# Three of the eight key/value units of the memory move: one into the differential attention's sub-layer norm, two round the query norm

## What is computed

```python
h = rmsnorm(x, g_mix_pre); proj = h @ w_in              # q, k, v, u
da = diff_attention(q, k, v, lam)                       # 4 heads, 2 blocks of 128 queries
da = rmsnorm(da, g_subln) * (1.0 - lam_init)            # the sub-layer norm, per head
mix = jnp.concatenate([da, po], axis=-1) @ w_out        # po: the pooled half, made earlier
x = x + rmsnorm(mix, g_mix_post)
hq = rmsnorm(x, g_x_pre)                                # the query norm
xq = (hq @ w_xq).reshape(b, s, X_HEADS, X_HEAD_DIM)
kv = (mem_n @ w_xkv).reshape(b, MEM_LEN, 2, X_HEADS, X_HEAD_DIM)   # depends on mem alone
sc = einsum(xq, kv[:, :, 0]); xo = einsum(softmax(sc), kv[:, :, 1])
```

## Time and profile before

| | before |
|---|---|
| median of 3 runs | 1147.33 us |
| the profiled execution, its own time | 1145.42 us |
| its span in the trace | 1143.6 us |
| PE busy | 1104.4 us (97%) |
| DVE busy | 628.3 us (55%) |
| ACT busy | 499.0 us (44%) |
| POOL busy | 33.2 us (3%) |
| mean granted TensorE clock | 0.994 of full speed |
| kv0 starts / first xq unit starts | 71.99 / 167.39 us from the span's start |

### The profile page before, as it was taken

The page is one execution under the profiler, slowest core; times in us unless marked ns, Lnnn a source line. Parts: engine busy times, 40 slices in busy tenths (PEclk is TensorE's granted clock), DMA queues, the critical chain, the costliest instruction groups (busy, mean ns, idle before and its releaser), DMA issues.

```text
span 1143.6 us, 18870 instructions
## 1 busy us (share of the span) xinstructions
PE 1104.4 (97%) x7892; PEld 1018.2 (89%) x7892; DVE 628.3 (55%) x831; ACT 499.0 (44%) x627; POOL 33.2 (3%) x47
## 2 busy tenths in 40 slices
PE   6999989999999999999999999999999999999997
PEld 6999779789999879988779999888999979999986
DVE  5765555364545445676565545446467565545542
ACT  5645455364444335554354444335532145444431
POOL 0100110000000001000010000000000010000000
PEclk9999989999999999999999999999999999999999
DMA  8833325334545546432135454554543233454530
GB/s 316 319 121 132 133 107 184 111 134 180 196 171 202 202 148 242 148 113 109 38 111 221 151 216 152 217 187 158 194 143 111 75 146 148 152 217 154 215 111 37
DMA packets 26718, 183.58 MB, mean 161 GB/s; under 512 B 3008, under 2 KB 3152, under 8 KB 5408
## 3 DMA queue, kind: packets, MB, share of 16 engines
q1 hardware_dynamic: 24912, 175.47, 42.4%
q0 software_dynamic: 1744, 7.20, 1.8%
HBM read 181.61 MB, written 1.05 MB: 160 GB/s over the span
## 4 chain that ended last, share of the span: by engine, by line
PE 92%; DVE 3%; ACT 2%; POOL 1%; issue 1%; DMA 1%; POOLq 0%; SPq 0%; DVEq 0%
PE G L1458 21%; PE G L1460 20%; PE G L1459 20%; PE D L1458 6%; PE D L1459 6%; PE D L1460 6%; PE D L1969 3%; PE D L1531 1%; POOL s_rstd L340 1%; PE D L1828 1%; PE D L1856 1%; ACT s_y L423 1%; DMA s_cst<-in_consts 1%; PE T L1841 1%; DVE s_xTl L841 0%
## 5 line engine op out<-in xcount | busy, mean ns | idle before, releaser
L812 DVE TENSOR_TENSOR s_wlo<-s_raw,s_whi 128x2048 fp32r<-128x2048 f32 (+1 forms) x165 | 371.8, 2276 | 179.5 <-ACT s_whi L412 179.5
L1458 PE MATMUL G<-s_xTh,s_whi 128*128 128x256 f32 x1448 | 408.7, 282 | 3.6 <-DVE s_xTl L841 3.6
L412 ACT ACTIVATE s_whi<-s_raw 128x2048 fp32r<-128x2048 f32 (+1 forms) x165 | 313.5, 1909 | 213.3 <-PE G L1460 108.0
L1460 PE MATMUL G<-s_xTh,s_wlo 128*128 128x256 f32 x1448 | 406.6, 281 | 0.0
L1459 PE MATMUL G<-s_xTl,s_whi 128*128 128x256 f32 x1448 | 405.9, 280 | 0.0
L1458 PEld LDWEIGHTS G<-s_xTh,s_whi 128*128 128x128 f32 x1448 | 272.0, 188 | 5.4 <-issue 5.2
L1459 PEld LDWEIGHTS G<-s_xTl,s_whi 128*128 128x128 f32 x1448 | 271.9, 188 | 1.0 <-issue 0.9
L1460 PEld LDWEIGHTS G<-s_xTh,s_wlo 128*128 128x128 f32 x1448 | 271.9, 188 | 0.1
L930 DVE TENSOR_TENSOR s_hb<-G,s_sg 128x512 f32<-128x512 f32 x33 | 22.8, 692 | 181.7 <-PE G L1460 145.3
L1458 PE MATMUL D<-s_whi,s_hTh 128*128 128x512 f32 x264 | 104.5, 396 | 0.0
L1459 PE MATMUL D<-s_wlo,s_hTh 128*128 128x512 f32 x264 | 104.1, 395 | 0.0
(11 more groups left out here) (309 smaller groups left out, 1134.2 us busy)
## 6 DMA issues: line engine op xcount, KB each, us to landing
s_raw<-in_stream SPq DMA_DIRECT2D x165, 1024.0 KB, 5.0
s_gb<-in_rows POOLq DMA_DIRECT2D x4, 512.0 KB, 4.1
s_xn<-in_x SPq DMA_DIRECT2D x2, 512.0 KB, 4.0
s_y<-in_mem POOLq DMA_DIRECT2D x1, 1024.0 KB, 11.5
s_w<-in_cmpw POOLq DMA_DIRECT2D x1, 1024.0 KB, 7.3
out<-s_y SPq DMA_DIRECT2D x4, 256.0 KB, 2.0
s_poolm<-in_poolm POOLq DMA_DIRECT2D x1, 768.0 KB, 15.1
s_retd<-in_retm POOLq DMA_DIRECT2D x1, 768.0 KB, 5.2
```

The source lines that it names most:

```text
L412: nc.scalar.activation(whi[:, u % RING, 0:n], raw[:, u % RING, 0:n], ACT.Copy)\
L812: nc.vector.tensor_tensor(wlo[:, u % RING, 0:n], raw[:, u % RING, 0:n], whi[:, u % RING, 0:n], ALU.subtract).then_inc(lo_ready, 1)
L1458: nc.tensor.matmul(out_, sh, mh, start=start, stop=False)
L1460: return nc.tensor.matmul(out_, sl, mh, start=False, stop=stop)
```

## The change

The units of the stream are reordered: kv0 to kv4, out0, out1, kv5, out2, out3, kv6, kv7, then xq as before. `sum_at` maps the four out units to their new places, `LATE_UNIT` the three late kv units.

- PE works through the attention in pairs of steps: four kv units (kv1 to kv4) instead of seven between eight steps, then out0 after the last transposes.
- kv5 runs between out1 and `head_transposes`, into bank T0. kv6 runs after out3 into D0, kv7 after the transposes of the query norm into D1. ACT copies each out in `late_kv_evac`, with a semaphore of its own, `kv_late`, that the first `x_scores` waits for.
- The query norm's transposes use D2, D3, T0, T1, and the two `keep_clock` matmuls ahead of them are gone.
- ACT and DVE do their steps in pairs too, with one split per pair, and the other splits are put at the places where the units now go.

```diff
-PHASES = [("in", 8), ("kv", 8), ("out", 4), ("xq", 4), ...
+PHASES = [("in", 8), ("kv", 5), ("out", 2), ("kv5", 1), ("out2", 2), ("kv6", 2), ("xq", 4), ...
...
 # ACT
-            for s in range(8):
-                if s < 7:
-                    kv_evac(s + 1)
-                act.wait_ge(sem("da_tr"), s + 1)
...
-                if s < 6:
-                    exps(s + 2)
-                if s < 7:
-                    split(kv0 + 1 + s + RING)
+            for h in range(4):
+                kv_evac(h + 1)
+                for s in (2 * h, 2 * h + 1):
+                    act.wait_ge(sem("da_tr"), s + 1)
...
+                if h < 3:
+                    exps(2 * h + 2)
+                    exps(2 * h + 3)
+                split(kv0 + 1 + h + RING)
 
             act.wait_ge(sem("da_nat"), 8)
...
-            split(BASE["out"] + RING)
+            split(sum_at("out", 0) + RING)
+            split(sum_at("out", 1) + RING)
+            late_kv_evac(5)
             for hp in range(2):
                 act.wait_ge(sem("da_T"), hp + 1)
...
-            split(BASE["out"] + 1 + RING)
+            split(LATE_UNIT[5] + RING)
             post_squares(0, "out", 2)
-            norm(2, BASE["out"] + 3, range(1, 4))
+            norm_squares(2, xn, lambda c: chunk(y, c), 1, range(1, 4))
+            split(sum_at("out", 2) + RING)
+            late_kv_evac(6)
+            norm_hi(2, xTh)
+            split(sum_at("out", 3) + RING)
+            split(LATE_UNIT[6] + RING)
+            late_kv_evac(7)
+            split(LATE_UNIT[7] + RING)
 # DVE
-            for s in range(8):
-                if s >= 1:
-                    da_copy(s - 1)
-                if s < 6:
-                    maxes(s + 2)
-                if s < 6:
-                    split(kv0 + 1 + s + RING)
-                    probs(s + 2)
+            for h in range(4):
+                if h >= 1:
+                    da_copy(2 * h - 2)
+                    da_copy(2 * h - 1)
+                if h < 3:
+                    maxes(2 * h + 2)
+                    maxes(2 * h + 3)
+                    probs(2 * h + 2)
+                    probs(2 * h + 3)
+                split(kv0 + 1 + h + RING)
+            da_copy(6)
             da_copy(7)
...
-            norm_rest(2, BASE["out"] + 3)
+            norm_mean(2, "x1", 1)
+            norm_diag("x1", 1)
+            split(sum_at("out", 2) + RING)
+            norm_lo(2, xTh, xTl)
+            split(sum_at("out", 3) + RING)
+            split(LATE_UNIT[6] + RING)
+            split(LATE_UNIT[7] + RING)
 # PE
+            def late_kv(j):
+                wait_unit(LATE_UNIT[j])
+                rows(LATE_UNIT[j], memTh, memTl, o=late_kv_bank(j)).then_inc(unit_done, 1)
...
-                if 2 <= n <= 4:
+                if 3 <= n <= 4:
                     keep_clock(o[3], 2)
...
-            for s in range(8):
-                if s < 7:
-                    unit(kv0 + s + 1, columns if s < 3 else rows, memTh, memTl)
-                else:
-                    pe.wait_ge(sem("da_max"), 8)
-                    sum_unit("out", 0, late=True)
-                if s >= 1:
-                    da_out(s - 1)
-                da_transposes(s)
-                if s < 6:
-                    da_scores(s + 2)
+            for h in range(4):
+                unit(kv0 + h + 1, columns if h < 3 else rows, memTh, memTl)
+                if h >= 1:
+                    da_out(2 * h - 2)
+                    da_out(2 * h - 1)
+                if h < 3:
+                    da_scores(2 * h + 2)
+                    da_scores(2 * h + 3)
+                da_transposes(2 * h)
+                da_transposes(2 * h + 1)
+            pe.wait_ge(sem("da_max"), 8)
+            sum_unit("out", 0, late=True)
+            da_out(6)
             da_out(7)
...
             sum_unit("out", 1)
+            pe.wait_ge(sem("da_nat"), 7)
+            late_kv(5)
             head_transposes(lambda t, h: un[:, t, P * h:P * h + P], (sem("da_normed"), 1), sem("da_T"), 2)
             for j in range(2):
                 pe.wait_ge(sem("da_lo"), j + 1)
                 sum_unit("out", 2 + j)
+            late_kv(6)
             norm_transposes(2)
+            late_kv(7)
...
                 if h == 0:
                     pe.wait_ge(sem("xT_ready"), 24)
+                    pe.wait_ge(sem("kv_late"), 3)
```

More of the change, by code:

```diff
@@ L49 @@
 GU, DN = 2 * (FF // 256), FF // 256
-PHASES = [("in", 8), ("kv", 8), ("out", 4), ("xq", 4), ("xo", 4), ("gu0", GU), ("dn0", DN),
+PHASES = [("in", 8), ("kv", 5), ("out", 2), ("kv5", 1), ("out2", 2), ("kv6", 2), ("xq", 4), ("xo", 4), ("gu0", GU), ("dn0", DN),
           ("ev", 14), ("eo", 4), ("gu1", GU), ("dn1", DN), ("od", 16), ("oo", 4),
@@ L65, with sum_at @@
 PAIRS = {"out": (2, 3, 0, 1), "xo": (0, 1, 2, 3), "eo": (2, 3, 0, 1), "oo": (0, 1, 2, 3)}
-N_OF = dict(PHASES)
+N_OF = dict(PHASES, out=4)
+LATE_UNIT = {5: BASE["kv5"], 6: BASE["kv6"], 7: BASE["kv6"] + 1}
+def sum_at(ph, j):
+    return BASE["out2"] + j - 2 if ph == "out" and j >= 2 else BASE[ph] + j
+LATE_KV = ("kv5", "out2", "kv6")
 POW_N = {"subln": 8, "gn": 8, "hg0": 8, "hg1": 8}
@@ L104, in bank_reads @@
     for name, count in PHASES:
-        if not name.startswith("gu") and name not in SUMS:
+        if not name.startswith("gu") and name not in SUMS and name not in LATE_KV:
             for j in range(min(max(u - at, 0), count)):
@@ L557, in kv_evac, with late_kv_evac @@
                     evac(kv0 + j, vx[:, :, 256 * (j - 4):256 * (j - 3)])
+            def late_kv_evac(j):
+                act.wait_ge(unit_done, LATE_UNIT[j] + 1)
+                nc.scalar.activation(vx[:, :, 256 * (j - 4):256 * (j - 3)], halves(late_kv_bank(j)[:]), ACT.Copy)\
+                    .then_inc(sem("kv_late"), 1)
             kv_evac(0)
@@ L562, in _ @@
             exps(1)
-            for s in range(8):
-                if s < 7:
-                    kv_evac(s + 1)
-                act.wait_ge(sem("da_tr"), s + 1)
[L567 to L571, removed]
-                if s < 6:
-                    exps(s + 2)
-                if s < 7:
-                    split(kv0 + 1 + s + RING)
+            for h in range(4):
+                kv_evac(h + 1)
+                for s in (2 * h, 2 * h + 1):
+                    act.wait_ge(sem("da_tr"), s + 1)
+                    if s >= 2:
+                        act.wait_ge(sem("da_out"), s - 1)
+                    n = P * (s % 2 + 1)
+                    nc.scalar.activation(aT[:, s % 2, 0:n], TB[s % 2][:, 0:n], ACT.Copy).then_inc(sem("aT"), 1)
+                if h < 3:
+                    exps(2 * h + 2)
+                    exps(2 * h + 3)
+                split(kv0 + 1 + h + RING)
             act.wait_ge(sem("da_nat"), 8)
@@ L1085, in _ @@
             mean_square("subln", ss[:, 32:40], P)
-            split(BASE["out"] - 1 + RING)
+            split(sum_at("out", 0) + RING)
             dve.wait_ge(rstd_ready, pow_at("subln") + 1)
@@ L1493, in gates, with rows @@
                 return ins
-            def rows(u, act_h, act_l, ready=None):
+            def rows(u, act_h, act_l, ready=None, o=None):
                 hi = whi[:, u % RING, 0:UNIT].rearrange("p (k n) -> p k n", k=KT)
@@ L1503, in rows @@
                         c = slice(P * t, P * t + P)
-                        ins = passes(G[bank(u)][:, 256 * t:256 * t + 256], (act_h[:, kt, c], act_l[:, kt, c]),
+                        ins = passes((G[bank(u)] if o is None else o)[:, 256 * t:256 * t + 256], (act_h[:, kt, c], act_l[:, kt, c]),
                                      (hi[:, kt, :], lo[:, kt, :]), kt == 0, kt == KT - 1)
@@ L1539, in sum_unit @@
                 act_l = xTl if act_l is None else act_l
-                u, last = BASE[ph] + j, N_OF[ph] - 1
+                u, last = sum_at(ph, j), N_OF[ph] - 1
                 wait_unit(u)
@@ L2087, in gate_up @@
         return np.stack([_wide(g), _wide(u)], 1).reshape(GU, P, UNIT)
+    kv, mix = _wide(i["w_xkv"]), _sum(i["w_out"], "out")
     def cols(w, *ranges):
```

13 lines of the change are left out of this document (8 added, 5 removed).

## The result

The changed kernel takes **1132.82 us** (median of 4 runs, 1132.45 to 1137.5) against 1147.19 us before (4 runs, 1145.37 to 1147.39). The ratio is 0.9891, with a 95% interval of 0.9866 to 0.9916: 1.1% less time. The forecast was 1137.5 us and 9.8 us gained, the range 1135.6 to 1140.9. One of the four runs took 1137.5 us, at a mean clock of 0.994; what slowed it is open.

A forecast was written before the change was run, and what follows sets the result against it. PE, busy for 1104.4 of 1143.6 us, was taken to bound the kernel, so gains come only where it waits or runs slowly. 2.31 + 1.66 + 5.9 - 0.1 = 9.8 us off 1147.33 gave 1137.5 us, range 1135.6 to 1140.9.

The forecast's parts named there:

- The wait of the fourth pair: Attention, h = 3: with no scores ahead, PE waits 0.5 to 0.6 us before that pair's transposes.
- The rule of swinging clocks: Trainium skill: frequent short PE idle times between matmul groups can swing the clock; by it 6.8 us gained, not 9.8.
- wait ahead of the head transposes: Sub-layer norm: out1 and kv5 together cover the norm's chain, so PE's wait goes, +2.31 us.
- out2 at full clock: Behind the sub-layer norm: without the long pause out2 takes 5.53 us instead of 7.19, +1.66 us.
- query norm, out3's end to `xq`: kv6 and kv7 cover the query norm, leaving only its transposes of the 9.98 us, +5.9 us.
- attention in pairs, kv1 to the end of out1, less the three units: Attention steps paired with fewer kv units: last pair waits, an old 0.47 us wait goes, net -0.1 us.
- chain of 8.55 us: Sub-layer norm: from the last `da_out`'s start to the end of the factor's multiplication, including 3.62 us for POOL's power.
- Low clock at both places: Rival: clock stays low at out2 and the first 16 query-norm transposes; 6.8 us gained, 1140.5 us, chance 0.12.
- Waiting pairs: Rival: 1 us more wait in three attention pairs and one clock drop; 5.1 us gained, 1142.2 us, chance 0.07.
- the slower ring: Rival: attention's loop of copies, exponentials and splits takes 10 us instead of 7; 2.7 us slower, 1150.0 us, chance 0.03.
- No cover: Rival: kv6 and kv7 cover nothing, as queued splits and copies delay the query norm equally; 1143.4 us, chance 0.04.

The follow-up runs named there:

- e6: Changed kernel with DVE's split of the third pair moved behind the two copies of the fourth: 1132.34 us, ratio 0.9891.
- e3: Kernel before the change, with only the attention put in pairs of steps, two kv units and two splits per pair: 1147.96 us, ratio 1.0027.
- e5: Changed kernel run again, unaltered: 1135.82 us, ratio 0.9908.
- e8: Kernel before the change, with DVE's split in the sub-layer norm moved behind the multiplication by the norm's factor: 1141.77 us, ratio 0.9974.
- e1: Changed kernel with kv5 taken out of the sub-layer norm and run after out3, ahead of kv6: 1137.99 us, ratio 0.9940.
- e2: Changed kernel with kv5, kv6 and kv7 all ahead of the head transposes, query norm and its clock keepers as before: 1139.45 us, ratio 0.9942.
- e7: Kernel of e6 with kv6 ahead of out2, kv7 alone after out3, and query-norm high and low parts ahead of the splits: 1132.98 us, ratio 0.9891.

## Why the prediction was right or wrong

**Right.** The gain came from the places named, by the means named. The sub-layer norm is covered, out2 runs at full clock, both halves of the query norm's transposes find their diagonals, `xq` does not wait, and the keepers' removal costs nothing. The diagonals are ready 144.48 + 0.29 - 141.29 = 3.5 and 6.0 us after out3 (forecast 3.9 and 6.4), and DVE's split ends 9.0 us after it (forecast 9.5). The wait of the fourth pair is 0.75 us (forecast 0.5 to 0.6), and it is the copy queued behind DVE's split, as e6 shows: PE gets there 6.6 us after the transposes before (forecast 6.5), and the chain takes 7.35 us (forecast 7.0). The rule of swinging clocks did not apply: with waits of 0.75 and 1.18 us the clock stayed at 1.00 through the whole stretch.

**Wrong, by size, inside the stretch** (9.8 forecast, 11.1 measured):

| term | forecast | measured |
|---|---|---|
| wait ahead of the head transposes | +2.31 | +2.31 |
| out2 at full clock | +1.66 | +1.54 |
| query norm, out3's end to `xq` | +5.9 | 9.98 - 3.49 = +6.5 |
| attention in pairs, kv1 to the end of out1, less the three units | -0.1 | 60.41 - 42.55 - 17.09 = +0.8 |

The measured terms come to 11.1. The query norm's term was short because I took 2.06 us for sixteen transposing matmuls from rows that run to the end of a last matmul; where the next work follows at once they cost 1.75. The attention's was short because I added the small matmuls of two single steps: 8.1 us per pair, measured 7.66 (87.00 to 94.66) and 7.79 (94.66 to 102.45). e3 has a gain of the same kind, 0.6 us per pair of steps. Grouped, the small matmuls change over to the large ones half as often; that the gain lies in the changeovers is my reading, which no run isolates.

**Wrong, by omission, behind the stretch.** The step that failed is that I costed the rest of the program at nothing. I read the granted clock only in the stretch that is rewritten. In the profile of before PE works at the lower level in three stretches, of which I explained two (a fourth, from 1141.3 us, lies behind its last matmul). The third, at 479 to 482.5 us, cost 1.7 us in the profiled execution before and was absent after. e5 shows that it can as well be present after: it then costs about 3 us. Such a stretch belonged in the range, on both sides. In the same way I carried a gain read from an execution of 1145.42 us over to a median of 1147.33 without asking what the 1.9 us between them were; after the change the same gap was 0.4 us. The 4.7 us between forecast and median are 1.4 from the terms up to `xq`, 1.7 from the third stretch and 1.5 from that gap. Without the last two the median would lie in the range.

**Luck.** The first comparison, 14.4 us, is flattered by it: the kernel before stood at 1147.19 in its four runs and at 1144.48 to 1144.73 in the 44 later ones, and the changed kernel's profile missed the third stretch. Beside each other on one chip (e5) they are 8.7 us apart in the medians, 1144.48 and 1135.82, and 10.0 in the shortest runs, 1142.98 and 1132.93. That 1135.82 lies inside the range is luck as well, since the kernel before had come down by 2.7 us too. Firmer are the 11.1 us of the stretch: from kv1 to `xq` it takes 76.59 us in both profiles of the changed kernel, against 87.64 in the one of before.

**Right for half a wrong reason.** I read POOL's 3.62 us as the price of the power and built the chain of 8.55 us on it. It is 1.65 us; the rest was DVE's split that starts just before it, at 137.37 against 137.54:

```profile
137.37 2.28 DVE L812 TENSOR_TENSOR s_wlo<-s_raw,s_whi 128x2048 fp32r<-128x2048 f32 x1
```

In the changed kernel the split starts 0.30 us after the power, the chain from `da_out(7)` to the product shrinks to about 7 us, and kv5 covers it with over 4 us to spare. My forecast did not suffer, since kv5 covers either. But the credit does: of the 2.31 us wait 1.98, and with them the low clock of out2, were to be had by e8's one line, for 0.6 us more ahead of out2.

**The rivals.** Low clock at both places: refuted, though e1 and e2 show that each of the two pauses brings it back alone. Waiting pairs and the slower ring: not in this kernel; e3 shows the ring at work once the pairs have two splits, 3.07 us of wait and a low clock behind it, 0.27% slower than before. No cover: refuted by the profile after, without a wait at either place, and by e2, where taking the cover away costs 6.6 us.

**Beyond the change.** e6 and e7 both hold 0.9891 of the time of before, where the changed kernel beside them has 0.9908; the intervals overlap, and by positions, counted from kv1, e6 is 0.5 us and e7 1.0 us ahead of it at `xq`.

## What to carry to other kernels

On a kernel bound by one engine, count a pause twice: once as the wait, once as the slow work behind it. Here 2.31 us of wait cost another 1.5, while waits of 1.18 us (the changed kernel) and 1.77 us (e8) cost only themselves. Read the granted clock over the whole span before forecasting, since a sparse stretch far from the change can be caught or missed by it, and give the range that width. And before covering a long wait with other work, ask whether each instruction in the chain takes its own time or its neighbour's: the same power took 1.65 us and 3.62 us by the place of one split.

## What the runs showed of the hardware

POOL's power on 128 x 8 numbers takes 1.65 us where no DVE instruction runs beside its start (e8), and 3.62 us where a DVE `tensor_tensor` of 2.28 us on two SBUF inputs starts 0.17 us before it (before, e3). The excess of 1.97 us is nearly the split's remaining 2.1 us. The second block has a pair in which the DVE instruction takes 1.22 us and starts 0.18 us before; the power takes 2.57 or 2.58 us in every profile, 0.9 us more than alone:

```profile
559.30 1.22 DVE L1344 TENSOR_TENSOR s_on<-s_on,s_rg 128x1024 f32<-128x1024 f32 x1
559.48 2.57 POOL L354 TENSOR_TENSOR s_rstd<-s_ms,s_cst 128x8 f32<-128x8 f32 x1 [137.38 <-DVE s_ms L845]
```

So the power was held back until the DVE instruction ended. This agrees with the Trainium skill, "SBUF — State Buffer", section "SBUF: two separate sides", by which such a DVE instruction that starts first holds the shared ports for its whole length. That section of the Trainium skill says the same of the other order, and there the trace does not agree: in the changed kernel the power starts first, and the split that starts 0.30 us after it takes its usual 2.29 us.

```profile
119.64 1.65 POOL L354 TENSOR_TENSOR s_rstd<-s_ms,s_cst 128x8 f32<-128x8 f32 x1 [74.13 <-DVE s_ms L845]
119.94 2.29 DVE L841 TENSOR_TENSOR s_wlo<-s_raw,s_whi 128x2048 fp32r<-128x2048 f32 x1 [0.38 <-ACT s_whi L426]
```

In all twelve profiles, between PE's first and last matmuls, every pause of 2.04 to 3.07 us was followed by the lower clock, and every one of 0.7 to 1.77 us by the full clock, unless a longer one stood within 3 us of it.

The granted clock of one and the same program differs between executions at the same instructions: 1.00 and 0.50 at 468 to 472 us in two profiles of the changed kernel. PE had no wait there in either. In the slow one the small matmuls had begun 3.3 us before the clock fell; in the other the same matmuls ran through at full clock, so they alone do not decide it.
